# Conditioning weights in units of 1024 by 512: two units share a PSUM bank, copied in two halves

## What is computed

```python
def adaln(cond, w, b):
    m = jax.nn.silu(cond) @ w + b          # w is 2048 x 12288 for each layer
    return [m.reshape(cond.shape[0], 6, 1, D_MODEL)[:, j] for j in range(6)]

sh1p, sc1p, g1p, sh2p, sc2p, g2p = adaln(c_ctx[None], w_ada[l], b_ada[l])   # prompt
sh1s, sc1s, g1s, sh2s, sc2s, g2s = adaln(c, w_ada[l], b_ada[l])             # sample
hp = rmsnorm(xp, norm_g[l, 0]) * (1 + sc1p) + sh1p      # hs the same
# layer 0: neighbourhood attention, layer 1: gated linear attention (GLA), on hp and hs
xp = xp + g1p * rmsnorm(yp, norm_g[l, 1])
mp = square(relu(modulate(xp, ...) @ w1_mlp[l])) @ w2_mlp[l]    # 2048 -> 8192 -> 2048
xp = xp + g2p * rmsnorm(mp, norm_g[l, 3])
```

## Time and profile before

| what | value |
|---|---|
| runs | 2575.51, 2580.29, 2580.41 us; median 2580.29 |
| the profiled execution | 2579.76 us, its span 2578.0 us |
| PE busy | 2513.9 us, 98% of the span |
| DVE, ACT, POOL busy | 53%, 41%, 4% |
| mean DMA rate | 246 GB/s |
| chain that ended last | PE 81%, DMA 9%, DVE 5%, ACT 3% |

### The profile page before, as it was taken

One profiled execution on the slowest core, in us unless ns is written; L12 is line 12 of the kernel. 1 busy time (PEld: TensorE's weight loads), 2 busy tenths in 40 slices (PEclk: granted clock), 3 DMA queues, 4 the chain that ended last, 5 costly groups with the idle time before them and its releaser, 6 DMA issues.

```text
span 2578.0 us, 37638 instructions
## 1 busy us (share of the span) xinstructions
PE 2513.9 (98%) x14850; PEld 2032.8 (79%) x14850; DVE 1366.6 (53%) x1496; ACT 1051.7 (41%) x1148; POOL 114.4 (4%) x164
## 2 busy tenths in 40 slices
PE   6899999999999999999999999999999999999998
PEld 3578888778878878878777777897787888888887
DVE  2244445476546546546555454565765465564665
ACT  3223344363324323323443365583633333343342
POOL 0020000000000000000000032200000000000000
PEclk8999999999999999999999999999999999999999
DMA  9988888958887878878886954458588656555554
GB/s 361 360 269 287 289 288 286 336 164 266 290 269 255 291 252 269 290 244 275 283 274 220 307 180 159 157 180 301 184 260 290 208 185 206 166 193 198 184 200 168
DMA packets 497463, 634.54 MB, mean 246 GB/s; under 512 B 12128, under 2 KB 378512, under 8 KB 496080
## 3 DMA queue, kind: packets, MB, share of 16 engines
q1 hardware_dynamic: 488672, 608.46, 70.7%
q0 software_dynamic: 6352, 23.31, 2.7%
q10 hardware_dynamic: 2336, 1.31, 0.2%
HBM read 623.90 MB, written 9.13 MB: 246 GB/s over the span
## 4 chain that ended last, share of the span: by engine, by line
PE 81%; DMA 9%; DVE 5%; ACT 3%; issue 1%; SPq 0%; POOL 0%; DVEq 0%; ACTq 0%
PE PS L1245 23%; PE PS L1246 11%; PE PS L1313 11%; PE PS L1315 10%; PE PS L1314 10%; PE PS L1272 4%; DVE WLO L1800 3%; DMA RAW<-in_w_qkvg_gla 2%; ACT WHI L1546 2%; DMA RAW<-in_w_o_na 2%; DMA RAW<-in_w_o_gla 2%; PE PS L1254 2%; PE PS L1256 1%; PE PS L1255 1%; DMA SCR<-in_w_ada 1%; DMA RAW<-in_w_qkv_na 1%
## 5 line engine op out<-in xcount | busy, mean ns | idle before, releaser
L1800 DVE TENSOR_TENSOR WLO<-RAW,WHI 128x2048 fp32r<-128x2048 f32 x384 | 878.5, 2299 | 758.7 <-ACT WHI L1546 750.0
L1546 ACT ACTIVATE WHI<-RAW 128x2048 fp32r<-128x2048 f32 x384 | 731.1, 1914 | 721.1 <-DMA RAW<-in_w_mlp 471.8
L1245 PE MATMUL PS<-HM,WHI 128*128 128x512 f32 x2560 | 912.1, 400 | 6.0 <-DVE SCR L2037 4.1
L1246 PE MATMUL PS<-HM,WLO 128*128 128x256 f32 x2560 | 717.7, 280 | 0.0
L1245 PEld LDWEIGHTS PS<-HM,WHI 128*128 128x128 f32 x2560 | 481.6, 188 | 137.5 <-issue 15.7
L1246 PEld LDWEIGHTS PS<-HM,WLO 128*128 128x128 f32 x2560 | 483.8, 189 | 0.2
L1313 PE MATMUL PS<-WHI,HID 128*128 128x512 f32 x1152 | 454.2, 394 | 5.2 <-DVE WLO L1800 5.2
L1314 PE MATMUL PS<-WLO,HID 128*128 128x512 f32 x1152 | 449.9, 391 | 0.0
L1315 PE MATMUL PS<-WHI,HID 128*128 128x512 f32 x1152 | 449.6, 390 | 0.0
L1313 PEld LDWEIGHTS PS<-WHI,HID 128*128 128x128 f32 x1152 | 217.0, 188 | 63.2 <-issue 18.9
L1315 PEld LDWEIGHTS PS<-WHI,HID 128*128 128x128 f32 x1152 | 217.0, 188 | 45.8
(11 more groups left out here) (238 smaller groups left out, 1895.4 us busy)
## 6 DMA issues: line engine op xcount, KB each, us to landing
RAW<-in_w_mlp SPq DMA_DIRECT2D x256, 1024.0 KB, 5.8
ADW<-in_w_ada SPq DMA_DIRECT2D x176, 1024.0 KB, 8.5
RAW<-in_w_qkv_na SPq DMA_DIRECT2D x48, 1024.0 KB, 6.9
RAW<-in_w_qkvg_gla SPq DMA_DIRECT2D x32, 1024.0 KB, 6.2
SCR<-in_w_ada SPq DMA_DIRECT2D x16, 1024.0 KB, 11.2
RAW<-in_w_o_na SPq DMA_DIRECT2D x16, 1024.0 KB, 7.2
RAW<-in_w_qkvg_gla SPq DMA_DIRECT2D x32, 512.0 KB, 4.7
RAW<-in_w_o_gla SPq DMA_DIRECT2D x16, 1024.0 KB, 6.7
```

What stands on the lines that cost most here:

```text
L1245: mm(bank[:, 0:2 * T2], hi[:, k, cols], act[:, kc, 0:2 * T2], start=first, stop=False)
L1246: return mm(bank[:, 0:T2], lo[:, k, cols], act[:, kc, 0:T2], start=False, stop=last)
L1546: actv(WHI[:, 2 * s + u, 0:n], RAW[:, u, 0:n], ACT.Copy).then_inc(hi_done, 1)
L1800: tt(WLO[:, 2 * s + u, 0:n], RAW[:, u, 0:n], WHI[:, 2 * s + u, 0:n].bitcast(f32), ALU.subtract).then_inc(lo_done, 1)
```

## The change

A unit is now 1024 rows by 512 columns, and two units in a row (a even, a + 1 odd) hold the upper and lower rows of the same 512 columns. Both accumulate in the whole bank ROWB.

- SP loads a unit as two transfers of 512 rows by 512 columns (again 1 MB each; each contiguous run in DRAM is 2 KB where it was 1 KB).
- PE makes per unit half as many products, each with 512 columns moving. Only the even unit waits for `row_ready`.
- ACT copies and stores a pair only after its odd unit, in two halves (`row_half`): copy 256 columns, wait for this copy, issue its two transfers, and the same for the other half. In the attention stage both halves come in the odd slabs, one right behind the other and ahead of `split_hi` of piece 0, into two different tiles (MROW and MROW_NA). In the MLP's feature slabs half 0 and half 1 go with the two slabs of the second of two loop steps. In output slabs with a whole pair they come at the end of the slab, and half 1 waits until half 0's transfers have landed, since both use MROW.
- A first-MLP group has 10 units in place of 9 (three output slabs have two each, the last has none), and the value slabs have one each in place of two. In all there are 80 as before.
- The sample stream is turned into four banks (psum 5, 7, 2, 3) where it was two (5, 7), so PE no longer waits for DVE between its second and third quarter.

```diff
-        GU = 2 * NB + 1
+        GU = 2 * NB + 2
-        A_WO1 = A_QKV1 + 2 * NB
+        A_WO1 = A_QKV1 + NB
-        PROMPT_TB, SAMPLE_TB = [psum[4], psum[6]], [psum[5], psum[7]]
+        PROMPT_TB, SAMPLE_TB = [psum[4], psum[6]], [psum[5], psum[7], psum[2], psum[3]]
-        PLAN_WO0, PLAN_WO, PLAN_V = ((0, 1), (2, 3), (4, 5), ()), ((0,), (1,), (2, 3), ()), ((0, 1), (2, 3), (4, 5), (6, 7))
-        PLAN_MLP = {GU: ((0,), (1,), (2, 3), (4,)), 2 * NB: ((0,), (1,), (2,), (3,))}
+        PLAN_WO0, PLAN_WO, PLAN_V = ((0, 1), (2, 3), (4, 5), ()), ((0,), (1,), (2, 3), ()), ((0,), (1,), (2,), (3,))
+        PLAN_MLP = {GU: ((0, 1), (2, 3), (4, 5), ()), 2 * NB: ((0,), (1,), (2,), (3,))}
...
+        AC = 2 * UC
+        MROW_NA = SCR[:, 3 * S4 - UC:3 * S4]
...
                 if r == LAST:
-                    ada_row(A_QKV0 + r)
+                    row_half(A_QKV0 + r - 1, 0)
+                    row_half(A_QKV0 + r - 1, 1, MROW_NA)
                 for x in heads:
                     turned_keys(x)
-                if r < LAST:
-                    ada_row(A_QKV0 + r, r == 0)
+                if r < LAST and r % 2:
+                    row_half(A_QKV0 + r - 1, 0, first=r == 1)
+                    row_half(A_QKV0 + r - 1, 1, MROW_NA, first=r == 1)
                 split_hi(m, s, UNIT, (0,))
-                store_row(A_QKV0 + r)
...
+                    row = UNIT_ROWS * odd + YC * u
+                    src = w_ada[layer, row:row + YC, ds(col, AC)].rearrange("(c p) n -> p c n", p=P)
+                    sp.dma_start(ADW[:, u, :].rearrange("p (c n) -> p c n", c=4), src).then_inc(ada_in[u], 16)
...
+                if not odd:
+                    pe.wait_ge(row_ready, a)
                 for u in range(2):
                     pe.wait_ge(ada_in[u], ada_loads(a))
+                    w = ADW[:, u, :].rearrange("p (c n) -> p c n", c=4)
+                    for j in range(4):
+                        end = mm(ROWB[32 * j:32 * j + 32, 0:AC], CS[:, UKC * odd + 4 * u + j, :], w[:, j, :],
+                                 start=(not odd and u == 0), stop=(odd == 1 and u == 1))
                     end.then_inc(ada0_used if u == 0 else ada_done, 1)
...
+            def row_half(a, half, tile=MROW[:, :], first=False):
+                act.wait_ge(ada_done, a + 3)
                 if not first:
+                    for x in range(2):
+                        act.wait_ge(row_out[x], rows_stored(a))
+                if half and tile is not MROW_NA:
+                    act.wait_ge(row_out[0], rows_stored(a + 2))
+                actv(tile, ROWB[:, UC * half:UC * half + UC], ACT.Copy).then_inc(row_ready, 1)
+                act.wait_ge(row_ready, a + half + 1)
                 for b in range(2):
+                    act.dma_start(mod_rows[ds(a + half, 1), :, b].rearrange("o h j n -> (o j) h n"),
+                                  tile[b:P:32, :].rearrange("p (h n) -> p h n", h=2)).then_inc(row_out[half], 16)
...
-            def out_slab(m0, n, ada=(), f=None, last=False, keys=0):
+            def out_slab(m0, n, pair=None, f=None, last=False, keys=0):
...
-                for a in ada[:1]:
-                    ada_row(a)
-                    store_row(a)
+                if pair is not None and not pair[1]:
+                    row_half(pair[0], 0)
...
                     split_hi(m + 2, 0, UNIT, range(2), keys)
-                for a in ada[1:]:
-                    ada_row(a)
-                    store_row(a)
+                if pair is not None and pair[1]:
+                    row_half(pair[0], 0)
                 if 0 < n < YN - 1:
                     more_squares(f, (("x0",), ("x1",))[n - 1])
+                if pair is not None:
+                    row_half(pair[0], 1)
...
-                    bank = SAMPLE_TB[g % 2]
+                    bank = SAMPLE_TB[g]
```

More of the change, by code:

```diff
@@ L247, in build_program, with finished_pair @@
         prompt_xn, sample_xn = sem("prompt_xn"), sem("sample_xn")
-        PLAN_WO0, PLAN_WO, PLAN_V = ((0, 1), (2, 3), (4, 5), ()), ((0,), (1,), (2, 3), ()), ((0, 1), (2, 3), (4, 5), (6, 7))
-        PLAN_MLP = {GU: ((0,), (1,), (2, 3), (4,)), 2 * NB: ((0,), (1,), (2,), (3,))}
-        def out_units(g, n, a, per):
-            return () if a is None else tuple(g * per + (a + NB + at) for at in PLAN_MLP[per][n])
+        PLAN_WO0, PLAN_WO, PLAN_V = ((0, 1), (2, 3), (4, 5), ()), ((0,), (1,), (2, 3), ()), ((0,), (1,), (2,), (3,))
+        PLAN_MLP = {GU: ((0, 1), (2, 3), (4, 5), ()), 2 * NB: ((0,), (1,), (2,), (3,))}
+        def finished_pair(first, plan):
+            odd = [at for at in plan if at % 2]
+            return None if first is None or not odd else (first + (odd[0] - 1), len(plan) == 2)
         mod_rows = nc.dram_tensor("mod_rows", [2 * ADA // UC, 2, 2, 4, P], f32, kind="Internal").ap()
@@ L872, in gla_vector @@
             link(nc.vector.memset(DEC2, 1.0))
-            dve.wait_ge(row_out, rows_stored(A_WO1))
+            for half in range(2):
+                dve.wait_ge(row_out[half], rows_stored(A_WO1))
             def log_gates(n):
@@ L1155, in ada @@
                     if q < len(plan):
-                        load_ada(first + plan[q], layer, (first + plan[q]) * UC - layer * ADA)
+                        at = first + plan[q]
+                        load_ada(at, layer, (at - at % 2) * UC - layer * ADA, at % 2)
                 return ada
@@ L1287, in step @@
                             banks_read()
-                        ada_rows(ada)
-            def stream(m, bodies, body, ada, a=0, filled=None, start=0, banks_read=None):
-                with pe.Fori(start, bodies) as i:
-                    for s in range(2):
-                        step(i * 2 + (m + s), s, body, i * ada + (a + s) if s < ada else None, filled, banks_read)
+                        ada_rows(ada, odd)
             def filled(f):
@@ L1489, in mlp_group @@
             def mlp_group(g, layer, m, a, f, per=2 * NB, norm=None):
-                with pe.Fori(0, NB) as i:
-                    for s in range(2):
-                        slab = g * (4 * NB) + i * 2 + (m + s)
-                        ada = g * per + i + a if s == 0 and a is not None else None
-                        step(slab, s, features_out(HM), ada, filled(f), modulated(2 * layer + 1))
+                with pe.Fori(0, NB // 2) as pair:
+                    for x in range(2):
+                        for s in range(2):
+                            slab = g * (4 * NB) + pair * 4 + (m + 2 * x + s)
+                            ada = g * per + pair * 2 + (a + x) if s == 0 and a is not None else None
+                            step(slab, s, features_out(HM), ada, x, filled(f), modulated(2 * layer + 1))
                 for n in range(YN):
@@ L1573, in round_hidden, with step @@
                          ACT.Copy).then_inc(hid_hi, 1)
-            def step(m, s, ada=None, hidden=None, prefetch=True):
-                if prefetch:
-                    split_hi(m + 1, 1 - s)
-                if ada is not None:
-                    ada_row(ada)
-                if hidden is not None:
-                    round_hidden(*hidden)
-                if ada is not None:
-                    store_row(ada)
-            def stream(m, bodies, ada, a=0, start=0):
-                with act.Fori(start, bodies) as i:
-                    for s in range(2):
-                        step(i * 2 + (m + s), s, i * ada + (a + s) if s < ada else None)
+            def step(m, s, pair=None, hidden=None):
+                split_hi(m + 1, 1 - s)
+                if pair is not None:
+                    row_half(pair, s)
+                round_hidden(*hidden)
             def square(x, f, n, b):
@@ L1757, in mlp_group @@
             def mlp_group(g, layer, m, a, per, complete=False, last=False):
-                with act.Fori(0, NB) as i:
-                    for s in range(2):
-                        slab = g * (4 * NB) + i * 2 + (m + s)
-                        ada = g * per + i + a if s == 0 and a is not None else None
-                        step(slab, s, ada, (g * KC + i * 4 + (layer * HID_GROUPS * KC + 2 * s), i, s))
+                with act.Fori(0, NB // 2) as two:
+                    for x in range(2):
+                        for s in range(2):
+                            slab = g * (4 * NB) + two * 4 + (m + 2 * x + s)
+                            pair = g * per + two * 2 + a if x and a is not None else None
+                            step(slab, s, pair, (g * KC + two * 8 + (layer * HID_GROUPS * KC + 4 * x + 2 * s),
+                                                 two * 2 + x, s))
                 m0 = g * (4 * NB) + (m + 2 * NB)
@@ L1765, in mlp_group @@
                 for n in range(YN):
-                    out_slab(m0, n, out_units(g, n, a, per), f, last and n == YN - 1)
+                    out_slab(m0, n, finished_pair(None if a is None else g * per + (a + NB), PLAN_MLP[per][n]), f,
+                             last and n == YN - 1)
                 if complete:
```

81 lines of the change are left out of this document (31 added, 50 removed).

## The result

The changed kernel takes 2609.28 us in the median of four runs (2607.87 to 2612.10); the kernel before, on the same chip, 2577.93. The ratio is 1.0123 (95% interval 1.0105 to 1.0140). The direction and the place were as forecast, the size was not: 2598.7 was named, with a range that ended at 2609.0. The profiled execution of the changed kernel is the one of 2607.87 us, span 2606.0; set against the span of 2578.0 before, 28.1 us have to be found (unrounded, 2606.04 less 2577.97).

What follows compares the result with a forecast made beforehand. PE was taken as the bound. Terms 17.4 + 1.5 - 0.8 + 0.9 + 0.9 - 1.0 = 18.9 us on 2579.76 gave 2598.7 us, 0.7% slower; forecast 2595 to 2604, range 2587 to 2609.

Steps and rivals of the forecast that it cites:

- The main term: Attention stage: copies and issues ahead of the split delay it 3.0 us, less slacks: 17.4 us, plus 1.5 for PE's clock.
- Rival A: Attention stage: the clock falls in every odd slab, seven more losses of 1.5 us, 2609; chance 0.10.
- B: Attention stage: the delay does not reach PE, as ACT dispatches on or the slacks have reserves; 2580; chance 0.08.
- C: Output slabs: larger runs remove 7.1 us of weight waits, stores land under 3 us, delay hidden as in B; 2571.9; chance 0.06.
- D: Attention stage: the delay reaches the next slab's start but not the keys, 11.0 us in place of 17.4; 2592.3; chance 0.14.
- The attention's output stage: Split 2.1 us late behind half 0's landing, less 1.2 for shorter loads: +0.9, bounds -1.2 and +2.1.
- The GLA's output stage: Ends with the same plan as the attention's output stage: +0.9 us, same bounds, -1.2 and +2.1.
- The end of the first MLP: Last slab loses its unit, whose load lay beside awaited pieces, but the held split comes in: -1.0 us, bounds -3.0 and +2.1.
- the other output slabs: First MLP's other output slabs, nine with a whole pair: nothing lost; 0 to 9 us if ACT's hold outlasted the next piece's landing.
- The held split: Output slabs with a whole pair: half 1 waits for half 0's stores to land, so the split is 2.1 us late.
- Units -0.8: PE's work in the 80 units: 1.85 us each against 1.86, 0.8 us less; bounds 0 and 1.6.
- Four banks 0: Sample stream at three norms: PE does not wait for DVE between quarters, DVE paces the stage: 0, bounds -0.3 and 0.

Runs made afterwards that it cites:

- the curve: Five kernels, the one before, the changed one and three with store issues moved around the split: loss per odd slab against the split's delay; delay less loss 0.65 to 0.68 us.
- the second tile's run: Changed kernel, but half 1 is copied into a tile of its own in output slabs with a whole pair: 2599.21 us, ratio 1.0082.
- the kernel with r = 1 repaired: Changed kernel with the four store issues behind the split in the attention stage's slab r = 1 alone: 2604.08 us, ratio 1.0104.

## Why the prediction was too low

- **The main term, right in mechanism, short by 2.4 us.** 18.9 us were put for the attention stage with its one fall of the clock; 21.3 came. The delay was 3.02 as computed. The slack ahead of the keys was read from starts as 0.87; the curve says 0.66. Five slabs lost 2.37 each and r = 13 lost 2.15, 14.0 together, where 12.8 was forecast. Slab 15 lost 1.3 (1.05 forecast), slab 17 1.65 (1.6). In r = 1 the stall was 2.40 in place of 2.0, since the first two issues there took 1.76 us and not 1.13 (the row below), and a stretch at half the clock followed: 4.0 by the experiment, 3.5 forecast. PE's two waits show as 0.99 and 0.77, 1.76 in sum, while the slab lost 2.37: the bracketed waits understate here, and the distance between two starts is the number to use.

```profile
185.07 1.76 ACTq L1553 DMA_DIRECT2D mod_rows<-MROW  x2
```

- **Rival A has the right time and is wrong.** It gave 2609 by a fall of the clock in every odd slab. The windows around the pair of r = 5 have it at 1.00 in the changed kernel:

```profile
256.00:260.00 4.00, 3.01 (x18) 2.38 (x17) 3.31 (x6) 1.07 (x5) 0.00 (x0) 1.00 0.40 131
260.00:264.00 4.00, 4.00 (x26) 3.53 (x25) 2.91 (x5) 2.14 (x2) 0.00 (x0) 1.00 0.67 230
264.00:268.00 4.00, 3.23 (x27) 1.48 (x26) 1.20 (x3) 2.24 (x3) 0.54 (x1) 1.00 0.73 231
```

- **B, C and D** fall with the curve; C needed the stores to land in under 3 us too, and they took 5.0 at its own place (535.23 to 540.23) and 5.2 at the end of the first MLP (1352.65 to 1357.88). The issues hold ACT: 1.13 us for two of them, and 1.26 of idleness put down to them. The Trainium skill (DMA: Bandwidth & Descriptors, Anatomy of one DMA) gives about 50 ns for a sequencer's dispatch, in a section on transfers that GpSimd issues; the prediction carried that figure over to ACT, and on ACT's queue this trace does not agree with it (1.13 us for two).
- **The attention's output stage: +1.1 for +0.9, by luck.** Both terms of the sum were too small. The split was 2.1 late, as computed (541.87 for a piece landed at 539.8), but the hold cost 4.2 us of the stage by the second tile's run, because the stall was 3.32 and the clock fell behind it. With the hold gone the stage is 3.1 shorter than before (117.4 against 120.5), where 1.2 was put down to shorter loads. About 1.6 of the 3.1 is the clock, which fell for some 3 us behind the 1.83 before and stayed up behind 1.74 here; that the rest is the shorter loads is not shown by a run of its own.
- **The GLA's output stage: +2.1 for +0.9.** Same terms: the hold cost 3.0, and without it the stage is 0.9 shorter than before. The stall grew from 1.26 to 2.82, past the lengths behind which I had seen the clock stay.
- **The end of the first MLP is the step that failed: +4.2 with the value slabs, -1.0 forecast.** Two terms of the sum meet here. For the last slab I put -1.0, because it loses its unit; the other output slabs I put at nothing, because two units in a value slab had made PE wait for no weights. The second holds for the first three groups: they lose 1.9 to 2.3 us each for the extra unit, and the four value slabs gain 8.6 for their four. It does not hold for the last group, which is 6.3 longer: beside it POOL's gains and tables are loaded, and the tables have a share in it; the rest of the cause is open. The plan alone cost about 4 (2581.23 us, ratio 1.0015, in the kernel that has nothing else of the change). The held split, which I had as a bound of +2.1, cost 5.3 by the second tile's run: the stall was 4.36, with half the clock for 6.8 us around its end. The two overlap.
- **Units -0.8:** right. The busy sum of their products fell from 155.0 to 154.1 us, and the distance from a unit to its next product is 1.855 us in the mean of 63 units, where it was 1.864; over 80 units that is 0.7. In the kernel's time it cannot be told.
- **Four banks 0:** right in the sum, wrong in its reason. The row that I read the earlier trace rows shows 32 products without a gap because the clock was at half there (0.50 until 556, of 550.72 to 557.60): PE was too slow to wait. Where it came back earlier, two banks made it wait 0.81 us.
- The second MLP with the end was 1.0 longer for no reason that I can show; the kernels with any change in this study have 730.1 to 730.6 there, with two at 729.1 and 729.2, the kernel before 729.5.

The sum: 2.4 + 0.2 + 5.2 + 1.2 + 1.0 in the stages and 0.8 for the units (whose gain is inside the stages' figures), less 1.6 of scatter in the start, is 9.2 us over the forecast in the profiled execution; the median lies 1.4 above it, 10.6 over. So the mechanism of the attention stage was right, and the step that failed is a size: the end of the first MLP, put at -1.0, with nothing for the slabs ahead of it, and measured at +4.2. That is more than half of the 9.2.

## What to carry to other kernels

On a queue that also computes, a DMA issue is an instruction with a duration (here 0.56 us) and belongs behind whatever the bounding engine waits for next; pairing halves does not make fewer of them, it bunches them. Before batching small stores, count what stands between the batch and the first awaited piece, and give each half its own buffer, so that no wait for a landing (5.2 us here) stands in a compute engine's order. And cost a moved load at the place it moves to, with what else is loaded there: the last group of the first MLP took some 4 us more for its extra unit than each of the three before it.

## What the runs showed of the hardware

PE's clock does not follow the length of a stall alone. At slab 17 six kernels, the changed one among them, have the same wait of 1.90 us for the same copy. In the changed kernel the clock stays up behind it:

```profile
445.00:447.00 2.00, 1.82 (x16) 1.85 (x17) 0.00 (x0) 0.74 (x6) 0.00 (x0) 1.00 1.00 378
```

in the kernel with r = 1 repaired it falls:

```profile
445.00:447.00 2.00, 2.00 (x11) 2.00 (x11) 0.00 (x0) 2.00 (x5) 0.72 (x1) 0.50 1.05 387
```

Three of the six show the one (from unit 17 to unit 18 it takes them 22.4 us) and three the other (23.9 to 24.0). A stall of 3.12 us left the clock at 1.00 once, one of 1.83 before took it down. So a price for the clock behind a stall of two or three microseconds is here a chance of 1.6 us or so, not a term. It can also be more: around the end of the stall of 4.36 the clock stood at half for 6.8 us, around those of 3.26 and 3.88 in two other kernels for 3.4.
